# One-hot return of expert outputs in two fp32r passes, and a last chunk that closes one column half early

## The reference, cut to what matters

```
def moe_swiglu(xn, router_w, w1, w3, w2):
    logits = (xt @ router_w).astype(jnp.float32)
    top_v, top_e = lax.top_k(logits, TOP_K)
    gate = jax.nn.softmax(top_v, axis=-1)
    ...
    def expert_block(args):
        xblk, e = args
        return (jax.nn.silu(xblk @ w1[e]) * (xblk @ w3[e])) @ w2[e]
    yb = lax.map(expert_block, (xb, block_e)).reshape(P, D)
    y = jax.ops.segment_sum(yb * slot_w[:, None], slot_tok, num_segments=N)
```

## Time and profile before

| what | value |
|---|---|
| median of three runs | 2207.64 us (2207.59 to 2208.37) |
| the profiled execution | 2205.92 us, its span 2204.2 us |
| mean granted TensorE clock | 0.974 |
| busy | PE 2084.8 us (95%), DVE 1638.7 (74%), ACT 1291.2 (59%), POOL 15.4 (1%) |
| the eight expert blocks | from about 1160 to 2180 us of the span, 127.3 us each |

### The profile page before, as it was taken

One profiled execution on the slowest core, in us unless ns is written; L12 is line 12 of the kernel. 1 busy time (PEld: TensorE's weight loads), 2 busy tenths in 40 slices (PEclk: granted clock), 3 DMA queues, 4 the chain that ended last, 5 costly groups with the idle time before them and its releaser, 6 DMA issues.

```text
span 2204.2 us, 33424 instructions
## 1 busy us (share of the span) xinstructions
PE 2084.8 (95%) x12896; PEld 1882.6 (85%) x12896; DVE 1638.7 (74%) x1694; ACT 1291.2 (59%) x1113; POOL 15.4 (1%) x71
## 2 busy tenths in 40 slices
PE   6998899989998998899989999999999999999997
PEld 5998899979998997899877888888888888888785
DVE  5888765544445988766558888798888888888885
ACT  4556454434434556345437767677777777677774
POOL 0000000000000000000000000000000000000000
PEclk8999999999999999999979999999999999999998
DMA  5544454435554534444438989899998989999893
GB/s 182 176 139 154 134 172 135 158 116 181 190 179 145 173 115 160 152 155 155 152 119 287 388 302 377 310 373 348 332 383 303 380 306 375 329 346 380 302 383 113
DMA packets 309485, 526.72 MB, mean 239 GB/s; under 512 B 13543, under 2 KB 156551, under 8 KB 309383
## 3 DMA queue, kind: packets, MB, share of 16 engines
q1 hardware_dynamic: 309382, 525.29, 68.1%
HBM read 524.21 MB, written 1.05 MB: 238 GB/s over the span
## 4 chain that ended last, share of the span: by engine, by line
PE 81%; DVE 9%; issue 4%; ACT 4%; DMA 0%; POOL 0%; DVEq 0%; ACTq 0%; SPq 0%
PE ps L1431 25%; PE ps L1433 24%; PE ps L1432 24%; DVE w_lo L966 2%; DVE c L1032 2%; ACT w_hi L645 2%; PE ps L1797 1%; PE ps L1742 1%; PE ps L1478 1%; PE ps L1809 1%; ACT w_hi L652 1%; PE ps L1545 1%; PE ps L1565 1%; DVE cacc L1016 1%; DVE xf L1050 0%
## 5 line engine op out<-in xcount | busy, mean ns | idle before, releaser
L966 DVE TENSOR_TENSOR w_lo<-raw,w_hi 128x2048 fp32r<-128x2048 f32 x330 | 751.9, 2281 | 374.0 <-ACT w_hi L645 311.9
L1431 PE MATMUL ps<-w_hi,a_hi 128*128 128x512 f32 (+1 forms) x1472 | 567.5, 386 | 1.8 <-DVE w_lo L966 0.9
L1433 PE MATMUL ps<-w_hi,a_lo 128*128 128x512 f32 (+1 forms) x1472 | 560.7, 381 | 0.0
L1432 PE MATMUL ps<-w_lo,a_hi 128*128 128x512 f32 (+1 forms) x1472 | 559.7, 380 | 0.0
L645 ACT ACTIVATE w_hi<-raw 128x2048 fp32r<-128x2048 f32 x159 | 301.5, 1897 | 313.2 <-PE ps L1433 305.3
L1431 PE MATMUL ps<-a_hi,w_hi 128*128 128x256 f32 x1520 | 442.9, 291 | 28.6 <-DVE a_lo L966 20.7
L1432 PE MATMUL ps<-a_lo,w_hi 128*128 128x256 f32 x1520 | 437.4, 288 | 0.0
L1433 PE MATMUL ps<-a_hi,w_lo 128*128 128x256 f32 x1520 | 437.1, 288 | 0.0
L652 ACT ACTIVATE w_hi<-raw 128x2048 fp32r<-128x2048 f32 x171 | 328.0, 1918 | 115.7 <-PE ps L1433 115.7
L1431 PEld LDWEIGHTS ps<-w_hi,a_hi 128*128 128x128 f32 x1472 | 276.6, 188 | 58.7 <-DVE w_lo L966 4.7
L1431 PEld LDWEIGHTS ps<-a_hi,w_hi 128*128 128x128 f32 x1520 | 299.5, 197 | 31.2 <-issue 23.1
(11 more groups left out here) (259 smaller groups left out, 2178.3 us busy)
## 6 DMA issues: line engine op xcount, KB each, us to landing
raw<-in_moe_w SPq DMA_DIRECT2D x171, 1024.0 KB, 6.4
raw<-in_w_in SPq DMA_DIRECT2D x68, 1024.0 KB, 5.2
mem_t<-in_moe_w SPq DMA_DIRECT2D x56, 1024.0 KB, 6.0
area<-in_moe_w SPq DMA_DIRECT2D x56, 1024.0 KB, 5.9
xf<-in_moe_w SPq DMA_DIRECT2D x56, 1024.0 KB, 5.6
raw<-in_ffn_w SPq DMA_DIRECT2D x33, 1024.0 KB, 5.2
raw<-in_w_mlstm_out SPq DMA_DIRECT2D x8, 1024.0 KB, 5.0
raw<-in_w_out SPq DMA_DIRECT2D x8, 1024.0 KB, 5.0
```

Of the source, the lines that this page charges most:

```text
L966: return dve.tensor_tensor(dst, whole, as_f32(hi), ALU.subtract)
L1431: pe.matmul(dst, wh, xh, start=start, stop=False, skip_group_check=True)
L1432: pe.matmul(dst, wh, xl, start=False, stop=False, skip_group_check=True)
L1433: return pe.matmul(dst, wl, xh, start=False, stop=stop, skip_group_check=True)
```

## The change

The spread is no longer made in plain fp32 from `y_tok` and the gated matrix. ScalarE now scales each half of `y` by the slot's gate on its way out of PSUM and writes it as fp32r (`y_hi_e`, in the tile `b_hi`); VectorE computes gate times `y` minus that (`y_lo_e`, in `b_lo`); TensorE multiplies both by the 0/1 matrix `sel_t` (in `b_hi`, fp32r), two matmuls where there was one. The gate of a slot comes from two matmuls of one column (`sel` stationary, the tokens' gates `gate_src` moving) and a copy to `gate_col`. `w2` chunks run over column halves outside and over k inside, and in the last chunk the first half signals `y_half` at its end.

```diff
@@ ScalarE, e_post @@
+                if m == N_EXP - 1:
+                    act.wait_ge(g_copied.sem, g_copied.at(b, 1))
+                    for n, s in enumerate((y_half, e_pe)):
+                        act.wait_ge(s.sem, s.at(b, (1, N_EXP)[n]))
+                        act.activation(y_hi_e[:, n * 512:(n + 1) * 512], ps[4 + n][:, :], ACT.Copy, scale=gate_col).then_inc(y_hi_done.sem, 1)
+                    return
...
-                    act.activation(g_slot, ps[7][:, 0:T], ACT.Copy).then_inc(g_copied.sem, 1)
+                    act.activation(gate_col, ps[7][:, T:T + 1], ACT.Copy)
+                    act.activation(sel_t, ps[7][:, 0:T], ACT.Copy).then_inc(g_copied.sem, 1)
...
-                if m == N_EXP - 1:
-                    act.activation(y_tok[:, 0:512], ps[4][:, :], ACT.Copy)
-                    act.activation(y_tok[:, 512:D], ps[5][:, :], ACT.Copy).then_inc(y_copied.sem, 1)
@@ VectorE, select @@
-                    ins = dve.tensor_scalar(sel_g[:, tt, :], iota_slot, rank, x_gate[tt][:, bass.ds(b, 1)], ALU.is_equal, ALU.mult)
+                    ins = dve.tensor_copy(gate_src[:, tt:tt + 1], x_gate[tt][:, bass.ds(b, 1)])
@@ VectorE, e_post @@
-                dve.wait_ge(e_pe.sem, e_pe.at(b, m + 1))
+                if m < N_EXP - 1:
+                    dve.wait_ge(e_pe.sem, e_pe.at(b, m + 1))
...
                 if m == N_EXP - 1:
-                    for n in range(4):
-                        dve.wait_ge(spread.sem, spread.at(b, n + 1))
-                        t = flat(h[:, 2 * n:2 * n + 2, :])
-                        dve.tensor_tensor(t, t, ps[(2 + n) % 4][:, :], ALU.add).then_inc(h_added.sem, 1)
+                    dve.wait_ge(g_copied.sem, g_copied.at(b, 1))
+                    for n in range(2):
+                        dve.wait_ge(y_hi_done.sem, y_hi_done.at(b, n + 1))
+                        c = slice(n * 512, (n + 1) * 512)
+                        dve.scalar_tensor_tensor(y_lo_e[:, c], ps[4 + n][:, :], gate_col, as_f32(y_hi_e[:, c]), ALU.mult, ALU.subtract).then_inc(y_lo_done.sem, 1)
+                    add_spread(b)
@@ VectorE, ahead of the blocks @@
+            dve.wait_ge(n_lo.sem, n_lo.moe)
+            dve.sem_inc(h_added.sem, 4)
             route()
             gather_lo(0)
-            dve.sem_inc(h_added.sem, 4)
@@ TensorE, e_chunk @@
-                    for k in range(2):
-                        for n in range(2):
+                    for n in range(2):
+                        for k in range(2):
                             c = slice(k * D + n * 512, k * D + (n + 1) * 512)
                             ins = three(ps[4 + n][:, :], xh[:, 2 * i + k, :], xl[:, 2 * i + k, :], wh[:, c], wl[:, c],
                                         g == 0 and i == 0 and k == 0, g == NGE - 1 and i == 1 and k == 1)
+                        if m == N_EXP - 1 and n == 0:
+                            ins.then_inc(y_half.sem, 1)
@@ TensorE, e_block @@
-                            ins = pe.transpose(ps[7][:, tt * P:(tt + 1) * P], sel_g[:, tt, :], ident[:, :])
+                            pe.transpose(ps[7][:, tt * P:(tt + 1) * P], sel[:, tt, :], ident[:, :])
+                        for tt in range(TT):
+                            ins = pe.matmul(ps[7][:, T:T + 1], sel[:, tt, :], gate_src[:, tt:tt + 1], start=(tt == 0), stop=(tt == 1), skip_group_check=True)
...
+            def spread_out(b):
...
                 for n in range(4):
+                    if n % 2 == 0:
+                        pe.wait_ge(y_lo_done.sem, y_lo_done.at(b, n // 2 + 1))
                     for i in range(2):
                         c = (2 * n + i) * P
-                        ins = pe.matmul(ps[(2 + n) % 4][:, i * T:(i + 1) * T], y_tok[:, c:c + P], g_slot, start=(i == 0), stop=True,
-                                        skip_group_check=True)
+                        dst = ps[SPREAD_BANKS[n]][:, i * T:(i + 1) * T]
+                        pe.matmul(dst, y_hi_e[:, c:c + P], sel_t, start=(i == 0), stop=False, skip_group_check=True)
+                        ins = pe.matmul(dst, y_lo_e[:, c:c + P], sel_t, start=False, stop=True, skip_group_check=True)
```

More of the change, by code:

```diff
@@ L97 @@
 E_AT = {key: m for m, key in enumerate(ESEQ)}
+SPREAD_BANKS = (2, 3, 0, 1)
 def bank_plan():
@@ L252, in trunk @@
         h_tok = q_t[:, :, :].rearrange("p (t k) n -> p t (k n)", t=TT)
-        y_tok = flat2(k_t)[:, 0:D]
+        y_hi_e, y_lo_e = (flat2(t)[:, 0:D] for t in (b_hi, b_lo))
+        sel_t = flat2(b_hi)[:, D:D + T]
+        gate_src, gate_col = flat2(k_t)[:, 0:TT], flat2(k_t)[:, 8:9]
         before = flat2(k_t)[:, D:D + P]
@@ L256, in trunk @@
         vflat = vx[:, :, :, :].rearrange("p a b c -> p (a b c)")
-        sel, sel_g = (vflat[:, i * T:(i + 1) * T].rearrange("p (t s) -> p t s", t=TT) for i in range(2))
-        g_slot = vflat[:, 2 * T:3 * T]
+        sel = vflat[:, 0:T].rearrange("p (t s) -> p t s", t=TT)
         x_hi, x_lo = (flat2(t)[:, 0:D].rearrange("p (k s) -> p k s", k=KB) for t in (a_hi, a_lo))
@@ L394, in trunk @@
         g_turned, g_copied = esig("g_turned", 1), esig("g_copied", 1)
-        y_copied = esig("y_copied", 1, 1)
+        y_half, y_hi_done, y_lo_done = esig("y_half", 1), esig("y_hi", 2), esig("y_lo", 2)
         spread = esig("spread", 4)
@@ L938, in _ @@
             gather_hi(0)
-            act.sem_inc(y_copied.sem, 1)
             with act.Fori(0, NE) as b:
@@ L1312, in gather_lo, with add_spread @@
                        x_hi[:, 4 * i:4 * i + 4, :].rearrange("p k s -> p (k s)")).then_inc(x_lo_done.sem, 1)
+            def add_spread(b):
+                for n in range(4):
+                    dve.wait_ge(spread.sem, spread.at(b, n + 1))
+                    t = flat(h[:, 2 * n:2 * n + 2, :])
+                    dve.tensor_tensor(t, t, ps[SPREAD_BANKS[n]][:, :], ALU.add).then_inc(h_added.sem, 1)
             def e_post(b, m):
                 kind, g, i = ESEQ[m]
-                dve.wait_ge(e_pe.sem, e_pe.at(b, m + 1))
+                if m < N_EXP - 1:
+                    dve.wait_ge(e_pe.sem, e_pe.at(b, m + 1))
                 if kind == "w3" and i == 1:
@@ L1752, in e_chunk @@
                         if g == 0:
-                            pe.wait_ge(y_copied.sem, y_copied.at(b, 0))
+                            pe.wait_ge(y_lo_done.sem, y_lo_done.at(b, 0))
                     xh, xl = hid_e[g % 2]
-                    for k in range(2):
-                        for n in range(2):
+                    for n in range(2):
+                        for k in range(2):
                             c = slice(k * D + n * 512, k * D + (n + 1) * 512)
@@ L1791, in e_block @@
                         gather_next(b)
-                pe.wait_ge(y_copied.sem, y_copied.at(b, 1))
+                spread_out(b)
+            def spread_out(b):
                 for n in range(4):
+                    if n % 2 == 0:
+                        pe.wait_ge(y_lo_done.sem, y_lo_done.at(b, n // 2 + 1))
                     for i in range(2):
                         c = (2 * n + i) * P
-                        ins = pe.matmul(ps[(2 + n) % 4][:, i * T:(i + 1) * T], y_tok[:, c:c + P], g_slot, start=(i == 0), stop=True,
-                                        skip_group_check=True)
+                        dst = ps[SPREAD_BANKS[n]][:, i * T:(i + 1) * T]
+                        pe.matmul(dst, y_hi_e[:, c:c + P], sel_t, start=(i == 0), stop=False, skip_group_check=True)
+                        ins = pe.matmul(dst, y_lo_e[:, c:c + P], sel_t, start=False, stop=True, skip_group_check=True)
                     ins.then_inc(spread.sem, 1)
```

## The result

The changed kernel took 2214.07 us (median of 14 runs, 2209.36 to 2214.77), the kernel before 2206.07 (14 runs beside them); the ratio (of the means) is 1.0035, 95% interval [1.0027, 1.0043]. That is 7.7 us slower by the means and 8.0 by the medians; 9.6 was forecast. The profiled execution took 2213.14 us, its span 2211.4, the mean granted clock is 0.968 where it was 0.974.

What follows compares the result with a forecast made beforehand. TensorE's instruction stream was taken to bound the blocks, with TensorE's queue and VectorE's third add ending the seam together. Seams 1.5 + gate column 3.6 + clock falls 4.5 = 9.6 us on 2207.6 gave 2217, range 2209 to 2223.

Steps and rivals of the forecast that it cites:

- the forecast's two larger causes: Clock falls at the seams between blocks, 4.5 us, and the gate column's narrow matmuls in TensorE's full stream, 3.6 us.
- The spread falls by 1.8 us: At each block's end, eight fp32 matmuls (3.72 us) become sixteen fp32r ones (1.92 us) on TensorE.
- The seam grows by 0.2 us: Between blocks, without expert work: 5.04 us becomes about 5.3, as VectorE's remainders precede its adds; 1.5 us at seven seams.
- The narrow matmuls cost 0.45 us: Two one-column fp32 matmuls per block, four records of 0.11 us in TensorE's full stream; 3.6 us over eight blocks.
- The clock falls at five of eight seams, 0.9 us each: TensorE's pause ahead of the spread grows to about 2.4 us and loses the clock at some seams; 4.5 us.
- the two rows of 1.98: Two 1.98 us TensorE pauses in the earlier trace: clock kept before 329.25, lost after the one before 979.36.
- The rival without falls: No seam loses the clock: 2212.7 us, from 2209 to 2213; chance 0.24.
- the one with long falls: Rival: the clock falls at all seams and holds long, 23 us slower, 2230; chance 0.07.
- VectorE gains half a microsecond in a stretch where TensorE doesn't wait for it.: In the selection, the second `tensor_scalar` per half (0.34 us) becomes a one-column copy; put among edits at nothing.
- The work behind the last block does "not move": After the last block: the fourth add ends at 1416.27 in both kernels, so the work behind it does not move.
- The earlier count of `h_added`: The earlier initial count sits before `route`, ahead of any use; put among edits at nothing.
- Faster if the remainders came first: Rival: VectorE takes the remainders before its split of chunk 1, or ends that split earlier; about 2198; chance 0.08.

Runs made afterwards that it cites:

- three experiments with the same pause: The changed kernel without the early half (2213.32 us), without the two narrow matmuls (2210.49 us), and with the long selection put back (2218.97 us).
- remainders first: The changed kernel with VectorE's two remainders and four adds ahead of its split of the next block's chunk 1: 2198.37 us, ratio 0.9964.
- filled: The changed kernel with eight idle fp32r matmuls of 512 columns in TensorE's pause ahead of the spread: 2211.1 us, ratio 1.0026.
- the gates made in the pause: The remainders-taken-first kernel with the selection's transposes and one-column matmuls moved to TensorE's pause ahead of the spread: 2190.92 us, ratio 0.9937.

## Why the prediction was nearly right

The measured 2214.07 us lies in the stated range, and the kernel became slower by the forecast's two larger causes. Part of the closeness is cancelling: one term was missing on the fast side and one on the slow side.

*The spread falls by 1.8 us.* It did: 2.02 us against 3.72. And it brought nothing by itself, as forecast, since VectorE's queue set the seam.

*The seam grows by 0.2 us.* It grew by 0.32 to 0.33. The step held (spread forecast 2.79 us after the last matmul's start, measured 2.80); the small miss is in two hand-overs: the first add 3.59 after it instead of 3.52, and TensorE 0.12 behind the end of the third add instead of 0.08.

*The narrow matmuls cost 0.45 us.* 0.46 by the rows, 0.43 by leaving them out. Halving the half-clock distance was right.

*The clock falls at five of eight seams, 0.9 us each.* It fell at five; four of them count, at 0.90, since the last lies in the tail: 3.6 us where 4.5 was forecast. The forecast counted seven seams for the waits but let all eight pay for a fall. That it was just five is luck (in three experiments with the same pause it was five, three and six); that a pause of 2.4 is lost at some seams and spared at others is what the two rows of 1.98 said. The rival without falls is out by the trace, and the one with long falls too: none lasted longer than 3.4 us while blocks followed, and the one of 10.2 us came behind the last.

*"VectorE gains half a microsecond in a stretch where TensorE doesn't wait for it."* This step was wrong, and it is the largest part of the miss. The full-block row showed TensorE busy at 126.08 of 127.33 us, and busy time of overlapping matmul records hid a wait of 0.4 us per block; the list of waits named it under the weight loads (3.0 us, seven times), which were not read. The shorter selection won back 0.30 per block by the chunks (0.33 in the kernel before without the gated matrix), 2.4 to 2.6 us in all.

*The work behind the last block does "not move".* VectorE's part doesn't: its fourth add ends 6.07 us after the last expert matmul's start, where it was 6.01. But the last stage begins 1.4 us later, with TensorE's stream now the last to get there by the profile, and the end comes 1.1 us later. This path was put at nothing. With it, 9.6 + 0.8 (seven seams, each 0.11 longer than forecast) - 0.9 (the falls) - 2.4 + 1.1 = 8.2 us; measured are 7.2 between the profiled executions, 7.7 between the means and 8.0 between the medians. In the traces the rest is the first block: its terms add 0.15 us (0.45 - 0.30), yet its last expert matmul comes 0.6 us earlier than before.

*The earlier count of `h_added`.* It was put down as ahead of any use. In fact TensorE waited 0.83 us for it at the first block of the kernel before; now it doesn't, and waits longer for the first remainder chunk behind it instead (1.97 us, where it was 0.88). The gain was given back within 10 us.

*Faster if the remainders came first.* The rival's place was right, its price somewhat high: it had a seam of 3.1 us and 9.9 us less than before, and with the order turned the seam is 3.73 and the time 7.7 us (0.36%) less. That both the rival and the run say 2198 is chance, as the rival started from 2207.6 and the run stands beside 2206.05.

## What to carry to other kernels

Before cheapening work on the engine that waits, look at what stands in the queue of the engine that will feed it: here two new instructions started 0.9 us after all of their data was there, and moving them and the adds ahead of one split of 2.3 us turned a loss of 0.35% into a gain of 0.36%. An early signal is worth nothing if its reader's queue is still busy when the late one would have come. Put small matmuls where the matmul engine pauses anyway, and read the waits of the weight loads apart from those of the matmuls: overlapping matmul records can cover a wait that happens in every block.

## What the runs showed of the hardware

The same pause of 2.41 to 2.42 us of TensorE, eight times in one execution, lost the clock five times and kept it three times. Every fall between two blocks lasted 3.4 us and cost 0.84 to 0.97 us, where matmuls running all of that time at half rate would have lost half of it, 1.7; the rest lay under the wait for VectorE (the seam with the fall from 1542.9 on is still 5.36 us long). At the seams, pauses of 1.2 us (kernel before) and 0.8 us (remainders first) and a pause with 0.6 us left of it (filled) never lost it, but one of 1.4 us ahead of the first block did in the kernel with the gates made in the pause. Ahead of the blocks, a pause of 3.95 us that ends at 449.2 kept the clock in the changed kernel (granted clock 1.00 from 440 to 455), where the same pause, ending at 449.7, lost it in the kernel before (0.77). So the length of a pause alone doesn't decide.

A plain fp32 matmul of one column costs nearly as much per record as one of 128: four records in 0.43 to 0.46 us here, 0.11 to 0.12 each, against 0.127 for the 128-column records of the earlier trace rows.
